# A decoder layer in float32: the first tile's second half and one block of x on GpSimd's queue, the other first loads regrouped

## What is computed

```python
def hybrid_token_mixer(x, w_in, gla_w_decay, gla_b_decay, gla_norm_g, w_out):
    B, T, _ = x.shape
    proj = x @ w_in
    (q_a, k_a, v_a, r_a, lr_a, q_b, k_b, v_b, gate_a, gate_b) = jnp.split(proj, IN_SPLIT_POINTS, axis=-1)
    ...
    y = jax.nn.sigmoid(gate_a) * y_a + jax.nn.sigmoid(gate_b) * y_b
    return y @ w_out
```

## Time and profile before

| | us |
|---|---|
| median of 3 runs | 1079.63 |
| lowest, highest | 1079.52, 1081.02 |
| the profiled execution, its own time | 1081.0 |
| its span | 1079.0 |
| PE busy | 1062.7 |
| DVE busy | 790.9 |
| ACT busy | 609.2 |
| POOL busy | 172.1 |
| DMA, whole span | 186.48 MB, 173 GB/s |

### The profile page before, as it was taken

One profiled execution on the slowest core, in us unless ns is written; L12 is line 12 of the kernel. 1 busy time (PEld: TensorE's weight loads), 2 busy tenths in 40 slices (PEclk: granted clock), 3 DMA queues, 4 the chain that ended last, 5 costly groups with the idle time before them and its releaser, 6 DMA issues.

```text
span 1079.0 us, 17958 instructions
## 1 busy us (share of the span) xinstructions
PE 1062.7 (98%) x5580; PEld 903.0 (84%) x5580; DVE 790.9 (73%) x1511; ACT 609.2 (56%) x1115; POOL 172.1 (16%) x119
## 2 busy tenths in 40 slices
PE   8999999999999999999999999999999999999996
PEld 6888888778888888888888999988888888888885
DVE  5457767677998998999999988876555555555556
ACT  4347545655556666666766666655555555444453
POOL 2040001203000012223324455510000000000001
PEclk9999999999999999999999999999999999999998
DMA  7555444444455554444444444445656555555553
GB/s 281 187 192 166 138 152 147 156 137 156 159 174 191 179 181 171 157 166 164 156 156 140 152 136 139 152 157 195 204 204 208 198 190 193 189 193 192 193 193 118
DMA packets 52857, 186.48 MB, mean 173 GB/s; under 512 B 6336, under 2 KB 6976, under 8 KB 52816
## 3 DMA queue, kind: packets, MB, share of 16 engines
q1 hardware_dynamic: 51152, 181.82, 49.5%
q0 software_dynamic: 944, 3.15, 0.8%
q10 hardware_dynamic: 720, 1.05, 0.3%
HBM read 184.94 MB, written 1.05 MB: 172 GB/s over the span
## 4 chain that ended last, share of the span: by engine, by line
PE 73%; issue 12%; POOL 6%; DVE 5%; ACT 2%; DMA 2%; POOLq 0%; ACTq 0%; SPq 0%; DVEq 0%
PE ps L1487 13%; PE ps L1583 10%; PE ps L1584 10%; PE ps L1585 10%; PE ps L1489 7%; POOL hot_j L461 5%; PE ps L1255 5%; PE ps L1257 5%; PE ps L1256 5%; PE ps L1538 3%; DVE wlo L789 2%; PE ps L1316 1%; ACT whi L484 1%; DMA xraw<-xT 1%; POOL xt L422 0%
## 5 line engine op out<-in xcount | busy, mean ns | idle before, releaser
L789 DVE TENSOR_TENSOR wlo<-raw,whi 128x1024 fp32r<-128x1024 f32 x341 | 427.5, 1255 | 238.9 <-ACT whi L484 236.3
L484 ACT ACTIVATE whi<-raw 128x1024 fp32r<-128x1024 f32 x343 | 363.2, 1060 | 283.7 <-DMA raw<-w_tiles_v 166.2
L1487 PE MATMUL ps<-pair,whi 128*128 128x512 f32 x1152 | 413.7, 401 | 0.1
L1489 PE MATMUL ps<-pair,wlo 128*128 128x256 f32 x1152 | 322.1, 280 | 0.0
L1487 PEld LDWEIGHTS ps<-pair,whi 128*128 128x128 f32 x1152 | 216.4, 188 | 48.0 <-issue 0.3
L1489 PEld LDWEIGHTS ps<-pair,wlo 128*128 128x128 f32 x1152 | 217.5, 189 | 0.0
L1583 PE MATMUL ps<-whi,hhi 128*128 128x512 f32 x512 | 199.4, 389 | 0.5 <-DVE wlo L789 0.5
L1584 PE MATMUL ps<-wlo,hhi 128*128 128x512 f32 x512 | 199.2, 389 | 0.0
L1585 PE MATMUL ps<-whi,hlo 128*128 128x512 f32 x512 | 199.2, 389 | 0.0
L461 POOL TENSOR_TENSOR hot_j<-raw_ij,gateT 128x512 f32<-128x512 bf16 x64 | 120.7, 1886 | 334.4 <-DVE raw_ij L1160 334.4
L672 ACT ACTIVATE low<-ps 128x256 f32<-128x256 f32 x144 | 55.1, 382 | 141.7 <-PE ps L1489 140.4
(11 more groups left out here) (212 smaller groups left out, 875.0 us busy)
## 6 DMA issues: line engine op xcount, KB each, us to landing
raw<-w_tiles_u SPq DMA_DIRECT2D x128, 512.0 KB, 3.2
raw<-w_tiles_v SPq DMA_DIRECT2D x128, 512.0 KB, 3.2
raw<-w_tiles_in SPq DMA_DIRECT2D x63, 512.0 KB, 3.2
raw<-w_tiles_q SPq DMA_DIRECT2D x16, 512.0 KB, 3.3
raw<-w_tiles_out SPq DMA_DIRECT2D x8, 512.0 KB, 3.3
xt<-x POOLq DMA_DIRECT2D x1, 1024.0 KB, 7.2
raw<-w_tiles_in SPq DMA_DIRECT2D x2, 256.0 KB, 3.9
xraw<-xT SPq DMA_DIRECT2D x2, 256.0 KB, 7.8
```

What stands on the lines that cost most here:

```text
L484: act.activation(whi[:, tile.slot, :], raw[:, tile.slot, :], ACT.Copy)\
L789: dve.tensor_tensor(wlo[:, tile.slot, :], raw[:, tile.slot, :], whi[:, tile.slot, :].bitcast(F32), ALU.subtract)\
L1487: pe.matmul(ps[:, bank, :], whi[:, tile.slot, cols], pair[:, k, :, :].rearrange("p a n -> p (a n)"), start=k == 0, stop=False)
L1489: last = pe.matmul(ps[:, bank, SEQ:2 * SEQ], wlo[:, tile.slot, cols], ahi[:, k, :], start=False, stop=k == KC - 1)
```

## The change

GpSimd's queue brings the second half of tile 0 and then x part 1. SP issues the first half, tiles 1, 2 and 3, and then the small tensors. ScalarE issues x parts 0, 2 and 3 at the start, and x part 4 after the second half of tile 0 has been copied. The semaphore of tile 0's first half is now `raw_full0`, that of the second half the new `raw_second`. The zeros for the warming matmuls are written by VectorE, ahead of its first `x_low`.

```diff
-X_PARTS, X_ON_ACT = 5, 3
+X_PARTS = 5
...
-        sp.dma_start(raw[:, 0, 0:CW], w_tiles_in[0, :, 0:CW]).then_inc(S["raw_first"], 16)
-        sp.dma_start(raw[:, 0, CW:], w_tiles_in[0, :, CW:]).then_inc(raw_full[0], 16)
-        load(Tile(1), w_tiles_in[1, :, :], wait=False)
-        for k in range(2, NS):
-            part = x_parts[k + 1]
-            sp.dma_start(xraw[:, part, :], xT[:, part, :]).then_inc(in_xT[k + 1], 16)
+        sp.dma_start(raw[:, 0, 0:CW], w_tiles_in[0, :, 0:CW]).then_inc(raw_full[0], 16)
+        for k in range(1, NS):
             load(Tile(k), w_tiles_in[k, :, :], wait=False)
...
-        pool.memset(zeros[:, :].bitcast(F32), 0.0).then_inc(S["zeros_ready"], 1)
+        pool.dma_start(raw[:, 0, CW:], w_tiles_in[0, :, CW:]).then_inc(S["raw_second"], 16)
+        pool.dma_start(xraw[:, x_parts[1], :], xT[:, x_parts[1], :]).then_inc(in_xT[1], 16)
...
-        for k in range(X_ON_ACT):
+        for k in (0, 2, 3):
             act.dma_start(xraw[:, x_parts[k], :], xT[:, x_parts[k], :]).then_inc(in_xT[k], 16)
...
-        for half, full in enumerate((S["raw_first"], raw_full[0])):
+        for half, full in enumerate((raw_full[0], S["raw_second"])):
             cols = slice(half * CW, (half + 1) * CW)
             x_high(half)
             act.wait_ge(full, 16)
             act.activation(whi[:, 0, cols], raw[:, 0, cols], ACT.Copy).then_inc(S["hi_first"], 1)
         act.sem_inc(S["hi_ready"], 1)
+        act.dma_start(xraw[:, x_parts[4], :], xT[:, x_parts[4], :]).then_inc(in_xT[4], 16)
...
+        dve.memset(zeros[:, :].bitcast(F32), 0.0).then_inc(S["zeros_ready"], 1)
         for half in range(2):
             cols = slice(half * CW, (half + 1) * CW)
             x_low(half)
```

More of the change, by code:

```diff
@@ L315, in layer @@
     OUTB = (6, 7, 0, 1)
-    names = ("raw_full0 raw_full1 raw_full2 raw_full3 raw_first zeros_ready hi_first lo_first in_xT0 in_xT1 in_xT2 in_xT3 in_xT4 in_lr in_x in_small "
+    names = ("raw_full0 raw_full1 raw_full2 raw_full3 raw_second zeros_ready hi_first lo_first in_xT0 in_xT1 in_xT2 in_xT3 in_xT4 in_lr in_x in_small "
              "in_ln1 in_ln2 hi_ready lo_ready lo_first_q tiles_used evac_act evac_dve consts "
```

## The result

| | us |
|---|---|
| before, median of 6 runs (lowest, highest) | 1080.33 (1079.21, 1081.44) |
| after, median of 6 runs (lowest, highest) | 1084.18 (1083.25, 1084.92) |
| ratio after to before, 95% interval | 1.0029 [1.0019, 1.0040] |
| the profiled execution of after, its span | 1084.3, 1082.6 |

The prediction was 1078.8, with a range up to 1081.2: the change was expected to gain 0.8 us and lost 3.9.

What follows compares the result with a forecast made beforehand. TensorE, 98% busy, was taken to bound the kernel, with tile 1's start carrying the change. Terms -0.8 +0 +0 took the profiled 1081.0 to 1080.2, or 1078.8 against the median 1079.63; range 1077.4 to 1081.2.

Steps and rivals of the forecast that it cites:

- What bounds the kernel: Whole span: TensorE busy 98%, about 16 us idle; everything behind tile 1 shifts by as much as its start.
- the one number that carries the change: Start of tile 1 on PE, 10.71 us before, forecast 9.9, 0.8 us earlier.
- GpSimd's first packet: Kernel start: first packet of GpSimd's queue at 3.0 us, 2.2 us after an issue at 0.81.
- the losing side: Kernel start: x1 landing from 7.8 us on makes the change a loss.
- shares about equally, 35 against 42: Earlier trace, transfer issued at 776.57: after 2.2 us GpSimd's packets share about equally with another queue's.
- x1's landing: Kernel start: x1, second in GpSimd's queue, lands at 7.0 us, chosen from its row of 5.3 us from issue.
- The lower end: x1's landing if its GpSimd transfer takes 3.6 us as when alone in its queue: 4.95 us.
- The upper end: x1's landing with first packet at 3.0 and a third of the packets per queue: 8.5 us.
- SyncE and ScalarE: Kernel start: w1 and x2 land at 7 to 8 and no longer gate; issuing x4 costs 0.2 us.
- the slower one: Rival at the first hole: clock falls, 1.7 us on top of 0.7, 1082.0; chance 0.12 including other late cases.
- Nothing moves: Rival at the start: same 1.5 MB needed, tile 1 within 0.3 us of 10.71, 1079.6; chance 0.13.
- GpSimd is prompt: Rival at the start: x1 lands at 5 to 6, 1.8 to 2.3 us gained, 1077.5; chance 0.15.

Runs made afterwards that it cites:

- the run with GpSimd alone: Changed kernel with SyncE and ScalarE issuing nothing until x1 has landed: 1083.9 us (1081.7 for the kernel before beside it).
- the run with PE kept busy: Changed kernel plus 14 unused matmuls on zeros between the two halves of tile 0: ratio to the kernel before 1.0007 [0.9998, 1.0017].
- the hole of 2.73: Changed kernel with half of the decay weights as second transfer on each of SyncE's and ScalarE's queues: ratio to the kernel before 1.0018 [1.0009, 1.0027].
- that of 2.94: Changed kernel with SyncE and ScalarE each issuing one transfer, then waiting for tile 0's second half: 1083.8 us against 1081.1 for the kernel before.
- holes of 2.04 (two runs): One is the changed kernel with x1 back on ScalarE's queue: ratio to the kernel before 0.9997 [0.9988, 1.0007]; the other is not identified.

## Why the prediction was wrong

**What bounds the kernel** held, with one thing missing. All the rest of the span is as long as before (1059.95 and 1059.6 us from the low-rank matmuls on). But the start of tile 1 is not the one number that carries the change: it moved by 2.88 us and the end of the first chunk by 3.94, as PE ran at 1.2 GHz behind it. In the table, the low-rank start is 8.3 to 8.4 us behind tile 1 wherever the clock stays up and no new hole comes; it is 9.4 after the change.

**GpSimd's first packet: the step that failed.** The prediction had it at 3.0, 0.81 plus the 2.2 us of the earlier trace rows. It came at 6.0. Part of it is the start of the issue (1.32, not 0.81): 0.5 us. The large part is that the 2.2 us were taken for a delay of GpSimd's own. Its own are 1.4, as the run with GpSimd alone shows. In the earlier trace rows SyncE's queue moves 102 of a tile's 144 packets in that time, and GpSimd's starts when the tile, which was issued 0.12 us ahead of it (776.45), is nearly through: the rest of the 2.2 us was a wait, and at the start of the kernel the same wait is 3.3 us. A second place in the kernel before shows it too, the transfer xt issued at 19.43; the DMA queues from 19.43 to 21.75, then from 21.75 to 22.5:

```profile
q1 hardware_dynamic: 118, 0.47, 59.5%
...
q0 software_dynamic: 39, 0.16, 59.8%
q1 hardware_dynamic: 26, 0.06, 19.4%
```

In 2.3 us not one packet of q0 beside 118 of q1, and then both; the tile ahead was issued at 19.29. Both places fit a wait for what was issued earlier. Had the row been read as a wait behind what is ahead, the working would have been: w0a and w1 (0.79 MB) on SyncE's queue and x0 and x2 (0.39 MB) on ScalarE's first. The kernel before has moved some 0.87 MB by 6.0 us and goes on at 340 to 377 GB/s, so these 1.18 MB are through at 6.8, and x1 comes after 9, on the losing side of every bound. The same row was read a second time for "shares about equally, 35 against 42", though the first quarter of a microsecond has 5 against 26 and the next 13 against 15: there the one queue takes over from the other. After the change the sharing did hold, 109 to 97 and 117, but only from 6.0 on.

The Trainium skill ("DMA: Bandwidth & Descriptors", section "Queues, rings and completion order") says that each DMA engine goes round the queues that have work, packet by packet. The trace agrees from 6.0 on and not before, unless GpSimd's queue had nothing yet for the engines; which of the two it is, no run here shows.

**x1's landing.** Bounds 4.95 and 8.5, taken 7.0, measured 9.8. The lower end was a GpSimd transfer beside idle hardware queues (measured: 4.8 with both held). The upper end lay too low, for it too began at 3.0. In it 256 packets were counted for w0b and x1; they were 128 in all, completions with them, as GpSimd's queue packs 4 KB into a packet where ScalarE's has 128 packets of 1 KB for x0. That error went the other way: with 6.0 as the start and 128 packets at the shares above, x1 comes at 6.0 + 128/109 x 2.5 = 8.9, still 0.9 short of the measured one. The value of 7.0 was taken from x1's own row, of a hardware queue. The run with x1 alone on GpSimd's queue shows what that was worth: 7.3 and 6.9.

**SyncE and ScalarE.** As said: ScalarE waited for x1 and for no other transfer up to tile 2; w1 landed at 1.26 + 6.2 = 7.5 and x2 at 1.27 + 6.4 = 7.7. The issue of x4 on ScalarE ran beside the copy and cost nothing (0.2 was taken), x4 did not gate (it landed at 9.90 + 3.8 = 13.7, just when ScalarE took it up). From x1's copy to tile 1 it was 2.55 us with the clock up (9.88 to 12.43 in the run with PE kept busy), where 2.9 was taken: x2's copy starts 0.84 us after x1's, and tile 1 then waits for PE's six matmuls of the second half, not for ScalarE. The zeros on VectorE start the warming 0.17 us later, within the 0.25, and cost nothing. None of these terms mattered.

**The rivals.** What happened is the slower one, by its own mechanism: from x1 above 8.0 the hole lets the clock fall. It fell 2.2 us after the last work, where the earlier trace rows has 2.3. That is not a fixed time: it was 2.6 with the hole of 2.73, and with that of 2.94 the clock fell 3.8 us after the last work, when PE had begun again. With holes of 2.04 (two runs) the matmuls stayed quick. Its price was put at 1.7 us, from the 3.6 us of work that PE needed at the start of the kernel before; measured 2.2 in the trace (2.4 in the times), since the clock stayed low through 5.1 us of work. That one row of 3.6 was at the short end: at the start of the other traces the matmuls are slow for 3.6 to about 6 us, and behind the holes for 3.3 to about 6 us. Two terms, then: x1's 1.75 instead of 0.7, and the clock's 2.2 instead of 1.7. It was given 0.09 to 0.12, because the row that could have told where x1 falls had been read as a latency.

*Nothing moves* was wrong: the amount moved by 6 us was not what held x1 (1.10 MB against 0.87 before), its queue was. *GpSimd is prompt*, with x1 below 6, was seen only where the other queues had nothing or one transfer each ahead (4.8 and 5.4).

## What to carry to other kernels

A delay between issue and first packet is not a property of a queue until what the other queues moved in that time has been counted: if what they were given earlier ends just as it starts, part of it was a wait, and that part grows with what stands ahead. A third queue for the loads that are needed first is worth little while the two others are full; put what is needed first where nothing is ahead of it. And where a hole on TensorE may grow beyond the largest after which the matmuls are seen to stay quick (2.04 us here), price the clock as well, from more than one row, or fill the hole.

## What the runs showed that was not expected

- GpSimd's first packet came when the first two transfers that SyncE's and ScalarE's queues were given, large or small, were most of the way through: 6.0 us with 0.79 and 0.39 MB in them, 4.6 with 0.52 and 0.39 MB, 3.1 with 0.28 and 0.15 MB, 2.9 with one each, 2.7 with none. Whether that is a number of transfers or simply what was issued before GpSimd's at 1.32 stays open; the second would also cover.
- The granted clock stayed at 0.50 from 9.2 to 16.0, though PE worked again from 10.9: 5.1 us of work, where the warming at the start of the kernel before took 3.6. With a hole of 3.83 us the matmuls were slow and the granted clock was shown as 1.00.
- The DMA engines have a stretch of 1 to 2 us at about half their rate or less, in nearly all runs, at no fixed time. With GpSimd's queue started at 3.1 they moved 94 GB/s from 4.0 to 4.5.
- Start times that differ by up to 1 us do not show in the medians: 18.4 to 20.0 for the low-rank matmuls went with ratios from 0.9983 to 1.0009, in no order.
